# Four mixed layers on one core: attention values held still while the turned probabilities stream past

## The reference, cut to what matters

```
o_c = einsum('bghtn,bgnd->bghtd', p_c, vc)                      # compressed keys
o_s = einsum('bghtl,bgtld->bghtd', p_s, vs_g)                   # selected blocks
o_w = einsum('bghtk,bgkd->bghtd', p_w, vw)                      # window
o   = gates[0] * o_c + gates[1] * o_s + gates[2] * o_w          # layers 0 and 1
o   = einsum('bhqk,bhkd->bhqd', p, v)                           # layers 2 and 3
mix = concatenate([o_a, o_b]) @ w_out                           # o_a: the recurrence
```

## Time and profile before

| | |
|---|---|
| median of three runs | 1466.06 us (1465.76 to 1473.11) |
| profiled execution, its own time | 1465.25 us |
| its span, first to last instruction | 1463.5 us |
| mean granted TensorE clock | 0.978 |
| PE busy | 1389.7 us, 95% |
| DVE, ACT busy | 976.4 us (67%), 700.4 us (48%) |

### The profile page before, as it was taken

One profiled execution on the slowest core, in us unless ns is written; L12 is line 12 of the kernel. 1 busy time (PEld: TensorE's weight loads), 2 busy tenths in 40 slices (PEclk: granted clock), 3 DMA queues, 4 the chain that ended last, 5 costly groups with the idle time before them and its releaser, 6 DMA issues.

```text
span 1463.5 us, 24482 instructions
## 1 busy us (share of the span) xinstructions
PE 1389.7 (95%) x10006; PEld 1285.3 (88%) x10006; DVE 976.4 (67%) x1660; ACT 700.4 (48%) x1149; POOL 85.1 (6%) x79
## 2 busy tenths in 40 slices
PE   9998899999999898999998999999999999999997
PEld 7997689999899777999987998889998899889996
DVE  5766775555759466655565685787768555786777
ACT  4755444334385543434344544455545454454453
POOL 0320000000014000000000011120000000000000
PEclk9999999999999899999998999999999999999999
DMA  8742245555443213655533434345454433445441
GB/s 317 276 150 87 87 147 195 177 192 183 166 155 137 91 59 121 225 175 195 178 131 142 145 116 145 134 163 183 180 200 159 173 123 132 157 157 206 187 173 58
DMA packets 38343, 233.22 MB, mean 159 GB/s; under 512 B 4984, under 2 KB 8776, under 8 KB 11864
## 3 DMA queue, kind: packets, MB, share of 16 engines
q1 hardware_dynamic: 36168, 224.18, 43.2%
q0 software_dynamic: 2064, 7.47, 1.6%
HBM read 230.55 MB, written 1.09 MB: 158 GB/s over the span
## 4 chain that ended last, share of the span: by engine, by line
PE 82%; DVE 10%; ACT 4%; issue 2%; POOL 0%; DMA 0%; SPq 0%; DVEq 0%; ACTq 0%
PE bank L746 24%; PE bank L747 24%; PE bank L748 23%; DVE w_lo L582 2%; PE bank L850 2%; ACT w_hi L572 1%; PE bank L930 1%; PE bank L952 1%; PE bank L954 1%; PE bank L953 1%; DVE a_lo L603 1%; DVE nstat L1555 1%; PE bank L826 1%; DVE arena L1630 0%; ACT a_hi L598 0%
## 5 line engine op out<-in xcount | busy, mean ns | idle before, releaser
L582 DVE TENSOR_TENSOR w_lo<-raw,w_hi 128x1024 fp32r<-128x1024 f32 x404 | 484.9, 1237 | 97.4 <-ACT w_hi L572 94.2
L746 PE MATMUL bank<-a_hi,w_hi 128*128 128x256 f32 x1856 | 530.0, 286 | 3.1 <-DVE w_lo L582 3.1
L747 PE MATMUL bank<-a_lo,w_hi 128*128 128x256 f32 x1856 | 525.9, 283 | 0.0
L748 PE MATMUL bank<-a_hi,w_lo 128*128 128x256 f32 x1856 | 525.8, 283 | 0.0
L572 ACT ACTIVATE w_hi<-raw 128x1024 fp32r<-128x1024 f32 x404 | 406.3, 1050 | 97.6 <-PE bank L748 89.6
L746 PEld LDWEIGHTS bank<-a_hi,w_hi 128*128 128x128 f32 x1856 | 356.4, 192 | 7.4 <-issue 4.4
L747 PEld LDWEIGHTS bank<-a_lo,w_hi 128*128 128x128 f32 x1856 | 356.5, 192 | 1.3
L748 PEld LDWEIGHTS bank<-a_hi,w_lo 128*128 128x128 f32 x1856 | 356.6, 192 | 0.0
L746 PE MATMUL bank<-w_hi,a_hi 128*128 128x256 f32 (+1 forms) x512 | 168.8, 330 | 16.3 <-DVE a_lo L603 15.5
L747 PE MATMUL bank<-w_lo,a_hi 128*128 128x256 f32 (+1 forms) x512 | 161.8, 316 | 0.0
L748 PE MATMUL bank<-w_hi,a_lo 128*128 128x256 f32 (+1 forms) x512 | 161.3, 315 | 0.0
(11 more groups left out here) (248 smaller groups left out, 1484.4 us busy)
## 6 DMA issues: line engine op xcount, KB each, us to landing
raw<-in_stream SPq DMA_DIRECT2D x201, 1024.0 KB, 4.9
bias_t<-bias_rows SPq DMA_DIRECT2D x6, 512.0 KB, 7.0
heads_buf<-in_w SPq DMA_DIRECT2D x2, 1024.0 KB, 7.9
gains<-in_w SPq DMA_DIRECT2D x2, 1024.0 KB, 10.0
gains<-in_ln_g POOLq DMA_DIRECT2D x4, 512.0 KB, 3.9
gains<-in_ln_b POOLq DMA_DIRECT2D x4, 512.0 KB, 5.7
gains<-in_rms_g POOLq DMA_DIRECT2D x3, 512.0 KB, 3.8
res<-in_xT SPq DMA_DIRECT2D x4, 256.0 KB, 5.2
```

The source lines that it names most:

```text
L582: dve.tensor_tensor(w_lo[:, i % PARTS, half_tile(h)], raw[:, i % SLOTS, half_tile(h)], w_hi[:, i % PARTS, half_tile(h)].bitcast(F32), ALU. ...
L746: pe.matmul(out, lh, rh, start=first, stop=False)
L747: pe.matmul(out, lh, rl, start=False, stop=False)
L748: return pe.matmul(out, ll, rh, start=False, stop=last)
```

## The change

The value step swaps its operands: 64 columns of values are now the loaded operand and the turned probabilities of a head, 256 tokens, the streamed one, so the result has channels on the partitions. The two heads of a pair write partitions 0 to 63 and 64 to 127 of the same bank. As the causal mask leaves the second half of the keys only to the second half of the tokens, the second matmul of a head streams 128 columns.

The row weights must then lie along the columns. `spread_weights` makes them with TensorE: a weight column repeated 64 times is the loaded operand, the identity the streamed one, eight matmuls of 128 columns for a group, put before the odd V. ACT copies the bank to SBUF (`turned_w`), and DVE multiplies the group by it. The reciprocals move from `mix` to a new `head_weights`, before the copies of the odd T. The step `oT` goes for all attention outputs (`mT` takes its place: ACT and DVE make the high and low parts straight from SBUF); it stays for the recurrence. `compressed_values` gives its result turned too, and its second half is copied out by ACT in place of DVE.

The order of steps is now a table for each layer, in place of the lists that layers shared.

```diff
-    if l < 2:
-        lead = halves("hf0", "hf1") + [("a", "hq0"), ("gates",), ("b", "hq0"), ("logs",), ("a", "hq1")]
...
+STEPS = {
+    0: """
...
+        heads, hid 3, ho 0, ho 1, b vsvw, hidT, a nq1, gtT, S 0, S 1, ho_out, kcv, b nq1, oT 0, T 0, phase
+        out, oT 1, out 0 0 0, V 0, S 2, T 1, out 0 0 1, V 1, S 3, out 1 0 0, T 2, S 4, phase out1, out 1 0
...
+    steps = [step.split() for step in STEPS[l].split(",")]
+    return woven([tuple(int(x) if x.isdigit() else x for x in step) for step in steps])
...
+            if step[1] % 2 == 1:
+                uses.append(((l, "W", step[1] // 2), "O"))
...
+        turned_w = [lev1[:, 0:512], gains[:, 1, 0:512]]
...
-                for i in pair(m):
-                    val = attn_io(l, i)[4]
-                    wait_drained(pe, (l, "T", i))
-                    pt = pT[:, i % 2, :]
-                    o0, o1 = [b[:, tt * S + i % 4 * DH:tt * S + (i % 4 + 1) * DH] for tt in range(NT)]
-                    pe.matmul(o0, pt[:, 0:P], val(0), start=True, stop=True)
-                    pe.matmul(o1, pt[:, P:2 * P], val(0), start=True, stop=False)
-                    pe.matmul(o1, pt[:, 2 * P:3 * P], val(1), start=False, stop=True).then_inc(pv_done, 1)
+                o = [b[DH * i:DH * (i + 1), m % 2 * S:(m % 2 + 1) * S] for i in range(2)]
+                val = [attn_io(l, i)[4] for i in pair(m)]
+                for i in range(2):
+                    wait_drained(pe, (l, "T", 2 * m + i))
+                    pe.matmul(o[i], val[i](0), pT[:, i, 0:S], start=True, stop=False)
+                for i in range(2):
+                    pe.matmul(o[i][:, P:S], val[i](1), pT[:, i, S:TRI], start=False, stop=True).then_inc(pv_done, 1)
+
+            def spread_weights(l, g):
+
+                b = open_bank((l, "W", g))
+                pe.wait_ge(w_ready, l * HEADS // 4 + g + 1)
+                half, h = head_of(l, 4 * g)
+                for i in range(2):
+                    for tt in range(NT):
+                        for odd in range(2):
+                            w = wgt[:, half, tt, h + 2 * i + odd:h + 2 * i + odd + 1].to_broadcast([P, DH])
+                            mm = pe.matmul(b[DH * odd:DH * (odd + 1), i * S + tt * P:i * S + (tt + 1) * P], w,
+                                           ident[:, :], start=True, stop=True)
+                close_bank(mm)
...
+            def mixed_high(l, r):
...
+                act.wait_ge(mix_done, mix_no(l, r))
+                act.activation(mixed_part(l, r)[0], mix_of(l, r).rearrange("p (i t) -> p i t", i=2),
+                               ACT.Copy).then_inc(mix_hi_done, 1)
...
+                    elif kind == "V" and step_[1] % 2 == 1:
+                        copy_out((l, "W", step_[1] // 2), turned_w[l // 2])
...
+            def mix(l, g):
+
+                key, wkey = (l, "V", g), (l, "W", g)
                 dve.wait_ge(pv_done, l * HEADS + 4 * g + 4)
...
+                wait_drained(dve, wkey)
+                whole = mix_of(l, 2 + g // 2 if l < 2 else g)
+                dst = mixed if l < 2 and g > 0 else whole
+                dve.tensor_tensor(dst, bank_of(key), turned_w[l // 2], ALU.mult).then_inc(*drained(key))
...
+                elif g == 3:
+                    dve.tensor_tensor(whole, whole, mixed, ALU.add).then_inc(mix_done, 1)
```

More of the change, by code:

```diff
@@ L67 @@
 HEAD_TILES = {0: ["hi0", "hi1"], 1: ["hi0", "hi1"], 2: ["v0", "v1"], 3: ["v0", "v1"]}
-def halves(*names):
-    return [(half, name) for name in names for half in ("a", "b")]
 def woven(steps):
@@ L89, in woven @@
     return out + highs + lows
-def out(r, tt):
-    return [("out", r, tt, hf) for hf in range(2)]
-def plan(l):
-    if l < 2:
-        lead = halves("hf0", "hf1") + [("a", "hq0"), ("gates",), ("b", "hq0"), ("logs",), ("a", "hq1")]
[L101 to L111, removed]
[6 rows of a table removed]
-                     + [("out", 2, 1, 1)])
-    if l == 2:
-        lead = ([("kw",)] + halves("qi0") + [("kwT",)] + halves("qi1") + [("kiT",)]
[6 rows of a table removed]
-    else:
-        lead = (halves("q0", "k0")
[4 rows of a table removed]
-    return woven([("phase", "tiles")] + lead
-                 + [("a", "v2"), ("S", 4), ("V", 3), ("b", "v2"), ("T", 4), ("a", "q3"), ("S", 5), ("V", 4), ("b", "q3")]
-                 + [("T", 5), ("a", "k3"), ("V", 5), ("oT", 0), ("b", "k3"), ("a", "v3"), ("S", 6), ("oT", 1), ("b", "v3")]
-                 + [("phase", "out")] + out(0, 0) + [("T", 6), ("S", 7)] + out(1, 0) + [("V", 6), ("oT", 2), ("T", 7)]
-                 + [("phase", "out1")] + out(0, 1) + [("V", 7)] + out(1, 1) + [("oT", 3)] + out(2, 0))
@@ L389, in build @@
         o_sq = [dec[1][:, 0:512], dec[1][:, 512:1024]]
+        o_full = [res[:, i // 2, i % 2 * 512:(i % 2 + 1) * 512] for i in range(4)]
         vc8 = res[:, 0, 512:1024].rearrange("p (h d) -> p h d", d=DH)
@@ L967, in turn_outputs @@
             def turn_outputs(l, r):
-                if l < 2 and r < 2:
-                    for tt in range(NT):
-                        wait_drained(pe, (l, "ho", tt))
-                else:
-                    wait_drained(pe, (l, "V", (2 * r - 3) if l < 2 else r))
-                    if l < 2:
-                        for tt in range(NT):
-                            wait_drained(pe, (l, "co", tt))
+                for tt in range(NT):
+                    wait_drained(pe, (l, "ho", tt))
                 b = open_bank((l, "oT", r))
@@ L1002, in add_output @@
             def add_output(l, r, tt, hf):
-                wait_drained(pe, (l, "oT", r))
+                if l < 2 and r < 2:
+                    wait_drained(pe, (l, "oT", r))
+                else:
+                    pe.wait_ge(mix_lo_done, mix_no(l, r))
                 if r == 0:
@@ L1104, in _ @@
                     elif kind == "V":
+                        if step[1] % 2 == 1:
+                            spread_weights(l, step[1] // 2)
                         values(l, step[1])
@@ L1506, in mix @@
                 if l < 2:
-                    step(dve.tensor_tensor(w, w, gates[:, :, 8 + 8 * half + h:12 + 8 * half + h], ALU.mult))
-                dve.wait_ge(pv_done, l * HEADS + 4 * g + 4)
-                key = (l, "V", g)
-                if l < 2 and g == 2:
-                    for tt in range(NT):
-                        wait_drained(dve, (l, "co", tt))
-                ps = bank_of(key).rearrange("p (t h d) -> p t h d", t=NT, h=4)
-                w = w.unsqueeze(3).to_broadcast([P, NT, 4, DH])
@@ L1526, in choose, with mixed_low @@
+            def mixed_low(l, r):
+                high, low = mixed_part(l, r)
+                dve.wait_ge(mix_hi_done, mix_no(l, r))
+                dve.tensor_tensor(low, mix_of(l, r).rearrange("p (i t) -> p i t", i=2), high.bitcast(F32),
+                                  ALU.subtract).then_inc(mix_lo_done, 1)
             def choose(n, times):
@@ L1853, in _ @@
                         turned_low(dve, (l, "oT", step_[1]), low, high)
+                    elif kind == "mT":
+                        mixed_low(l, step_[1])
                     elif kind == "kcv":
```

105 lines of the change are left out of this document (74 added, 31 removed), and 16 rows, old and new, of tables (lead, levels).

## The result

The changed kernel took 1459.94 us in the median of 7 runs (1456.91 to 1466.85), the kernel before 1467.66 in 7 beside it: ratio 0.9944, 95% interval 0.9922 to 0.9965. Forecast were 1457 and 0.9938. So the total is right.

What follows compares the result with a forecast made beforehand. TensorE's own work bounds layers 2 and 3, chains through DVE and ACT partly layers 0 and 1. Layers 0 to 3 give -3.5 + 0.5 - 2.9 - 3.0 = -8.9 against 1465.25: 1456.4, as a median 1457; range 1447 to 1468.

Steps and rivals of the forecast that it cites:

- TensorE's list: TensorE's own work in all layers: V -9.6, neighbours -3.2 and -1.2, spreading +14.4, oT -5.3, together -4.9 us.
- Rival A: V and spreading: column halves don't run together with 64 loaded columns, +35 us, 1492; chance 0.06.
- Layer 3: Layer 3: TensorE's saving of 1.55 counts in full and two waits of 0.7 are covered, -3.0 us.
- Layer 2: Layer 2: TensorE's saving of 1.55 counts in full and `kiT`'s wait of 1.3 is covered, -2.9 us.
- the new links lie under half tiles: Layers 2 and 3: head weights on DVE and ACT's copy of W are covered; a V without cover costs 0.2 to 0.8.
- Waits, layer 0: Layer 0: opening -3.1, low clock -0.5, late wait +0.8, half of TensorE's -1.3; together -3.5 us.
- DVE ends the recurrence's output at 118.7 as before (S 0 comes later but S 1 follows at once): Layer 0's opening: the recurrence's output ends no later, so the low part is ready at 121.5 in place of 125.7.
- the 3.1: Layer 0's opening: us saved before the first output product, waits of 3.0 and 1.9 becoming one of some 2.
- the danger at V 6: Late layer 0: V 6's bank waits for ACT's copy of W 2 behind S 7's exponentials, +0.8 us with hops.
- half of the -1.3 counts: Layer 0: half of TensorE's saving of 1.3 us there shortens the layer.
- a growing idle time of layers 0 and 1: Sign for layers 0 and 1: if their idle grows, the forecast is wrong.
- Rival B: Layers 0 and 1: ACT's copy of W delays V 6 and copies of T more than priced, +5 us, 1462; chance 0.30.

Runs made afterwards that it cites:

- experiment 1: The new operations with the old order of steps in all four layers, against the kernel before: 1463.65 us, ratio 0.9962.
- experiment 7: Changed kernel, but the eight matmuls of each spreading fill one column half, then the other: 1465.61 us, ratio 0.9987 to the kernel before.
- experiment 2: The old operations in the new order of steps, against the kernel before: 1468.43 us, ratio 0.9995.
- experiment 6: Changed kernel with T 3 ahead of `cs` in layers 0 and 1: 1458.04 us, ratio 0.9940 to the kernel before.
- experiment 9: experiment 6 with layer 0's steps from T 4 to the end in layer 1's order: 1456.64 us, ratio 0.9909 to the kernel before.
- experiment 8: Changed kernel without ACT's copy of the spread weights; DVE multiplies by what stands in the tile from earlier: 1459.02 us, ratio 0.9937 to the kernel before.
- experiment 5: Changed kernel with weights widened by a DVE copy after a small reciprocal and turned by four transposes: 1463.08 us, ratio 0.9963 to the kernel before.
- experiment 12: experiment 9 with layer 0's opening in layer 1 too and weights widened on DVE in layer 3 alone: 1454.48 us, ratio 0.9894 to the kernel before.

## Why the prediction was right, and where it was wrong

**TensorE's list: right.** V 0.99 for 1.04, W 0.87 for 0.9, a neighbour of another kind 0.2, as forecast. With the measured prices the list comes to -7.0, not -4.9, and in layers 2 and 3, less their idle time, TensorE does save 2.1 and 2.0 us for 1.55 forecast. That the swap pays by itself is not shown: experiment 1, where the order is left out, is 4 us faster in the median and no faster at equal clock. The rule of the Trainium skill (page TensorE: Matmul & The Clock Gate, section "Part 3: Packing small matmuls — row/col tiling"), that weight loads overlap running matmuls only when the row group differs, would leave a load for a column half bare. It did not hold in these runs. With 64 loaded columns the pairs of passes start 0.01 us apart and follow each other at 0.11, though a load is recorded at 0.15 in the mean; and experiment 7, which takes the pairing away, is 0.49 a spreading slower. Rival A is out.

**Layer 3: right** (-3.4 for -3.0), waits of 0.7 gone where the steps stand in front of them. **Layer 2: nearly** (-2.3 for -2.9); the wait of 1.3 is gone as forecast, but it missed a wait of 1.7 at W 1 behind the choice of keys. The step "the new links lie under half tiles" forgot that DVE is busy there.

**Layer 0: wrong.** Three things in "Waits, layer 0" failed.
- "DVE ends the recurrence's output at 118.7 as before (S 0 comes later but S 1 follows at once)" is the step that failed at the opening. S 1 can't follow at once. It needs one of two banks that DVE has to empty: a wait of 2.0 in every kernel with this order, old operations too (experiment 2). The output ended at 121.1. From there to the first output product it is 4.9 us, before 7.0, forecast 2.8. So of the 3.1 nothing was left: that product comes 0.5 later.
- I put the danger at V 6 and priced it 0.8; V 6 waits 0.2 (before 1.6). The danger was at S 5 and W 1. There a chain that begins with `cs` bounds the layer, and of the new operations the head weights stand *in* it (S 5 starts 0.3 later) and W directly behind the wait. With V's saving that is some 0.9 of the 3.5 that experiment 1 loses in this layer; the rest, an estimate by difference, is the lower clock, which now lies behind the wait. Moving T 3 out of the chain (experiment 6) takes both waits away; its layers are 0.9 and 1.7 shorter.
- T 6 directly behind S 7 waits 2.3 for its bank; experiment 9 takes it away. That kernel's layer 0 is 3.0 shorter, in part by its clock.

The common error: I spread TensorE's saving evenly ("half of the -1.3 counts"). As I read these traces, in a layer bound by chains what is saved beside the chain counts nothing, and what is added on it counts in full, and double where the lower clock is granted. The prediction had named a growing idle time of layers 0 and 1 as a sign that it is wrong, and that sign came.

**Rival B** had the right size and the wrong mechanism. Waits in layers 0 and 1 did grow (idle of layer 0 from 12.4 to 13.8 us, of layer 1 from 12.8 to 14.2), but they stay when ACT's copy of W is left out (experiment 8).

**Why the sum is right all the same.** The misses of layers 0 and 1, 7 us, should have put the result at 1464. In the profiled executions 2.8 came back outside the four stretches, 2.3 of it where a low clock happened to be gone, and 3.3 come from the step to the medians. Behind both stands, as far as the runs show, the clock: over all runs the mean granted clock is 0.9760 for the kernel before (35 runs) and 0.9796 after (7). The runs of before at 0.974 have a mean span of 1468.9 us (6 of them), those at 0.979 of 1464.6 (7), 0.9 us for each 0.001, so the 0.0036 are worth some 3 us. The rest holds at equal clock: at 0.979 those seven have spans of 1463.8 to 1465.3, the changed kernel's one run 1459.0, the old order with the new operations 1465.0. So some 5 us belong to new operations and new order together. Why the changed kernel is granted more isn't settled. So the hit is in part luck.

One slip in the prediction's sums: the chances for "faster" that it adds up, 0.28, 0.08 and 0.16, make 0.52, not 0.54.

## What to carry to other kernels

Before pricing an edit, mark for each stretch whether TensorE's list or a chain bounds it; an operation added on the chain behind a wait costs its full time, and twice that if the lower clock is granted there. Ask on which side of the wait the low clock lies, and compare kernels at equal clock before a gain of a few us is put down to an edit. For each step that is moved ahead, ask which step filled its bank last and when that bank is emptied: two equal steps in a row with a ring of two or three banks are a wait. And where a table sets the order of DVE's work through TensorE's, a long chain on DVE should be put behind the copies that TensorE needs next.

## What the runs showed of the hardware

- Span follows granted clock: in 35 runs of one kernel from 1459.8 us at 0.981 to 1472.4 and 1473.7 at 0.971, and one run of experiment 5, at 0.634, took 2271.48 us. Most of the spread between runs is that. One run doesn't fit: in experiment 12, 0.94 is recorded beside a span of 1451.1 us.
- A low clock ahead of a wait that another engine ends can cost nothing: before, 3.4 us of it ahead of S 5 left S 5 at 6.55 us behind `cs`; after, with none of it there, S 5 came at 6.88.
- The two column halves of TensorE behave like two queues: in experiment 7, where eight passes for one half are issued ahead of the other's, the first of the other half started 0.006 us behind the fifth of the first.
- Stepping from full-array products to a step on column halves and back costs some 0.33 us: V takes 0.99 beside streams of 0.66. S and V side by side save 0.2 of that (1.84 for 1.04 + 0.99).
- DVE's reciprocal costs 6.5 ns a column (3.34 us for 512), seven times a copy that repeats its input 64 times (0.47); for 8 columns it takes 0.20.
